# Where the arena begins in SBUF: from a multiple of 128 bytes to 64 bytes behind one

## Time and profile before

| what | value |
|---|---|
| runs shown | 2211.77, 2220.5, 2219.2 us; median 2219.2 |
| the profiled execution | 2212.16 us, its span 2210.4 us |
| TensorE's granted clock, mean | 0.985 |
| TensorE busy | 2096.7 us (95%) |
| VectorE, ScalarE busy | 779.8 us (35%), 627.7 us (28%) |
| read from HBM | 722.44 MB, 327 GB/s over the span |

### The profile page before, as it was taken

One profiled execution on the slowest core, in us unless ns is written; L12 is line 12 of the kernel. 1 busy time (PEld: TensorE's weight loads), 2 busy tenths in 40 slices (PEclk: granted clock), 3 DMA queues, 4 the chain that ended last, 5 costly groups with the idle time before them and its releaser, 6 DMA issues.

```text
span 2210.4 us, 27209 instructions
## 1 busy us (share of the span) xinstructions
PE 2096.7 (95%) x12031; PEld 1305.4 (59%) x12031; DVE 779.8 (35%) x1144; ACT 627.7 (28%) x988; POOL 42.9 (2%) x75
## 2 busy tenths in 40 slices
PE   9999999899898999989999899889999999999999
PEld 9986543333333443424333333327988998988997
DVE  8984211011010111111011011016666665876663
ACT  6664110000000000000000000005555444865442
POOL 3201000000000000000000000000000000000000
PEclk9999999999999999999999999999999999999999
DMA  7549999999999999999999999997444655544653
GB/s 239 169 137 372 425 429 429 429 429 429 429 429 430 429 430 429 429 428 428 430 429 429 430 429 429 429 427 262 147 168 148 214 191 188 193 172 149 204 191 114
DMA packets 146816, 725.27 MB, mean 328 GB/s; under 512 B 8711, under 2 KB 106555, under 8 KB 119691
## 3 DMA queue, kind: packets, MB, share of 16 engines
q1 hardware_dynamic: 145512, 721.53, 81.4%
q0 software_dynamic: 640, 1.37, 0.2%
q10 hardware_dynamic: 546, 0.63, 0.1%
HBM read 722.44 MB, written 1.07 MB: 327 GB/s over the span
## 4 chain that ended last, share of the span: by engine, by line
PE 66%; DMA 26%; DVE 5%; ACT 1%; issue 1%; SPq 0%; DVEq 0%; ACTq 0%
PE bank L1425 23%; PE bank L1287 18%; DMA weight_ring<-in_w_up_dram 10%; DMA weight_ring<-in_w_down_dram 10%; PE bank L1373 8%; PE bank L1250 5%; DMA weight_ring<-in_w_gate_dram 4%; PE bank L1456 3%; DVE weights_ring L2517 1%; DVE arena L2577 1%; PE bank L1093 1%; PE bank L1214 1%; PE bank L1642 1%; PE bank L1772 1%; PE bank L1665 1%
## 5 line engine op out<-in xcount | busy, mean ns | idle before, releaser
L1287 PE MATMUL bank<-weight_ring,arena 128*64 128x506 f32 x3024 | 633.1, 563 | 56.9 <-DMA weight_ring<-in_w_up_dram 42.5
L1287 PEld LDWEIGHTS bank<-weight_ring,arena 128*64 128x64 f32 x3024 | 219.0, 135 | 453.6 <-issue 359.3
L1373 PE MATMUL bank<-weight_ring,arena 128*64 128x512 f32 x1408 | 334.5, 628 | 36.4 <-DMA weight_ring<-in_w_down_dram 36.4
L2953 DVE TENSOR_TENSOR weights_ring<-weight_ring,weights_ring 128x2048 fp32r<-128x2048 f32 x110 | 249.7, 2289 | 127.2 <-ACT weights_ring L2211 126.8
L1373 PEld LDWEIGHTS bank<-weight_ring,arena 128*64 128x64 f32 x1408 | 102.5, 143 | 247.3 <-issue 194.3
L1425 PE MATMUL bank<-input_high,weights_ring 128*128 128x256 f32 x1920 | 242.6, 279 | 0.6 <-issue 0.6
L1425 PEld LDWEIGHTS bank<-input_high,weights_ring 128*128 128x128 f32 x1920 | 229.2, 188 | 2.7 <-issue 2.4
L2211 ACT ACTIVATE weights_ring<-weight_ring 128x2048 fp32r<-128x2048 f32 x109 | 205.7, 1909 | 61.0 <-DMA weight_ring<-in_w_ffn_down_dram 40.4
L2910 DVE TENSOR_TENSOR arena<-arena,bank 128x512 f32<-128x512 f32 x48 | 33.0, 688 | 498.2 <-PE bank L1250 498.2
L2105 ACT ACTIVATE arena<-bank 128x506 f32<-128x506 f32 (+1 forms) x48 | 23.5, 562 | 375.2 <-PE bank L1287 375.2
L1425 PE MATMUL bank<-input_low,weights_ring 128*128 128x256 f32 x960 | 129.4, 277 | 0.0
(11 more groups left out here) (432 smaller groups left out, 2079.1 us busy)
## 6 DMA issues: line engine op xcount, KB each, us to landing
weight_ring<-in_w_down_dram SPq DMA_DIRECT2D x62, 2816.0 KB, 21.8
weight_ring<-in_w_up_dram SPq DMA_DIRECT2D x60, 2816.0 KB, 19.5
weight_ring<-in_w_gate_dram SPq DMA_DIRECT2D x59, 2816.0 KB, 18.8
weight_ring<-in_w_ffn_gu_dram SPq DMA_DIRECT2D x44, 1024.0 KB, 5.1
weight_ring<-in_w_ffn_down_dram SPq DMA_DIRECT2D x22, 1024.0 KB, 4.9
weight_ring<-in_w_in_dram SPq DMA_DIRECT2D x16, 1024.0 KB, 6.3
arena<-in_w_xkv_dram SPq DMA_DIRECT2D x8, 2048.0 KB, 21.7
weight_ring<-in_w_gate_dram SPq DMA_DIRECT2D x10, 1408.0 KB, 10.0
```

Of the source, the lines that this page charges most:

```text
L1287: last = pe.matmul(bank[first_bank + c][MPAD * half:MPAD * half + MPAD, 0:(hi - lo) * HF], xs3[:, s, :], w[:, lo:hi, HF * half:HF * half + ...
L1373: last = pe.matmul(bank[6][MPAD * half:MPAD * half + MPAD, :], hidT[:, at:at + MPAD], W[:, j * D + 512 * half:j * D + 512 * half + 512], s ...
L2953: dve.tensor_tensor(low_slot(k), raw_slot(k), high_slot(k), ALU.subtract).then_inc(S("weights_low"), 1)
```

## The change

The padding ahead of the arena grows from 24 to 40 columns, from 96 to 160 bytes per partition. Every address of the arena, and of what is laid over it, rises by 64 bytes. Nothing else is different.

```diff
         RW = sb("router_w", KT * 16)
         small = sb("small", 184)
-        sb("arena_offset", 24)
+        sb("arena_offset", 40)
         Z = sb("arena", ARENA)
```

## The result

| | before | after |
|---|---|---|
| median of 10 executions | 2217.23 us (2210.87 to 2220.5) | 2225.61 us (2224.43 to 2227.12) |
| the profiled execution, its span | 2212.16, 2210.4 us | 2224.93, 2223.1 us |
| granted clock, mean | 0.985 | 0.986 |

The change makes the kernel slower by 8.4 us between the medians. That is just inside the 0.5% that the prediction set as what can be told from no change, but ten executions of each tell it apart.

The account below looks back on a forecast made before the run. It took weight transfers to bound the expert stage and TensorE the last stage. All terms were 0, so no change from the profiled 2212.16 us; the median was put at 2216 us, range 2203 to 2233 us.

Parts of the forecast that it names:

- What bounds each stage: Expert stage bound by weight transfers at 429 GB/s, last stage by TensorE multiplications one for one; first 250 us mixed.
- Transfers: Loads into the arena, mostly eight of 2048 KB in the expert stage: 0, bounds ±0.5 us.
- VectorE and ScalarE: Their arena accesses, in the last stage and first 250 us: same speed at both phases, 0, bounds ±2 us.
- full fp32: TensorE multiplications of L1642 and L1772: 379 ns whether operands share a phase modulo 128 bytes or not, so 0.
- the expert stage's slack: TensorE's waits for transfers there, 56.9 us before L1287, cover any slower multiplication: 0, or 6 us without cover.
- Rounded fp32: Last-stage TensorE multiplications of 256 and 512 columns, in_part, token_part and others: taken as 0 between bounds.
- The upper bound: Most the last stage's rounded multiplications could lose: +9.7 us for in_part, +3.3 us for 512 columns.
- Slow everywhere: All in_part multiplications of the last stage at the slow pace: 2880 x 0.75 x 4.5 ns = +9.7 us.
- The first rival: L1425, 256 columns: in_part falls into the slow pace, +13.0 us, 2229 us; chance 0.19, 0.16 over the bound.
- its worse form: In_part slow plus a further 4.5 ns on all 3456 multiplications of 256 columns: +27 us, chance 0.05.
- The second rival: Last stage: equal phases give back half the overhead of 256- and 512-column multiplications, 19 us, 2197 us; chance 0.12.
- The third: Last stage: slow stretches of in_part and token_part become fast, nothing else; -5.8 us, 2210 us; chance 0.07.

Follow-up runs that it names:

- second profile of before: Unchanged kernel profiled once more, nothing changed against before: one execution, 2214.75 us.
- The last experiment: Changed kernel with input_high and input_low moved to distance 192 from the ring, everything else at 0: 2209.13 us, 0.9975 of the kernel before.

## Why the prediction was wrong

**What bounds each stage: right.** Of 12.7 us between the spans the last stage has all, one for one as foretold. No wait grew; one of 1.0 us in the profile of before was missing in that of after, as in the second profile of before.

**Transfers, VectorE and ScalarE, full fp32, the expert stage's slack: right at 0.** 429 GB/s; 684 and 687 ns; 379 ns twice; 1127.66 against 1127.39 us. L1772, whose operands did change their distance, has 379 ns in the profiles of all six distances.

**Rounded fp32: wrong, and this is the step.** It reads "Between them I take 0, since the rows that do compare the phases (fp32, 512 columns) show nothing." The runs put +14.1 us in its place: in_part +15.6, token_part +1.1, 512 columns -2.6. Three things were wrong in it. The rows it trusted were of the kinds that hardly care: full fp32 does not move by a nanosecond, and 512 columns at 230 ns move by 1 to 3 ns, where 256 columns at 113 move by up to 6.7. The nearest row in kind and size, token_part at 117.5 ns, was named and not taken. And two paces at one address were read as "the phase does not fix the pace". It does not fix it at distance 192; at 0 it does, at 120.0.

**The upper bound was too low in one term and wrong in sign in another.** "Slow everywhere" was priced at before's slow pace, 117.9 ns, +9.7 us for in_part; it was +15.6, since the new pace was one that no row of before showed. The share of three quarters at the fast pace was right (2133 of 2880). The 512 columns, bounded at -1.6 to +3.3 us, gave -2.6: also mixed_high, counted as untouched, gained 3 ns.

**The first rival was the case that came.** In_part did become slow everywhere. Its +13.0 us meets the 13.1 of the last stage, by errors that cancel, which is luck: 5.9 us too little for in_part and 5.9 too much for the 512 columns; token_part's 1.1 us was not in it, nor the 1.0 us of the wait that went. The sign given for it, 2.83 us for 24, did not come either; it was 2.88, which no rival had. The price of its worse form, +27, is also mis-added: 13.0 and 3456 x 4.5 ns = 15.6 are 28.6. Its 2229 us did not come out, because it was laid on 2216, a guess at the median. An execution at the median already has a long run at the slow pace, and loses less. Laid on the profiled execution, 2212.16 + 13.0 is 2225.2, and 2225.61 was measured. The range (2203 to 2233) held the time; the likeliest case, no change, did not happen.

**The second rival** (equal phases let both streams pass) is refuted for 256 columns and true in small for 512: of 17 ns lost on each, 3 came back. **The third**, all fast, is not what the change does. The last experiment came nearest to it, with other addresses: both long runs are fast and 2267 of in_part's 2880 multiplications start the next one after 113 or 114 ns, but shorter stretches at 117.8 ns stayed.

**The rule of the Trainium skill** (SBUF — State Buffer, Who interferes with whom), that PE has two independent read ports and never waits on anyone, was read by the prediction as exactly 0 for this change. The section speaks of one engine against another, and there the trace agrees: the pace did not move with what VectorE, ScalarE and the DMAs did. It says nothing of where PE's own two operands lie against each other, and that cost 6.7 ns per multiplication. Whether its two reads are as independent as it says for rounded fp32, no run here shows directly, but the dependence speaks against it.

## What to carry to other kernels

Where a chain of short rounded multiplications (256 columns) bounds a kernel, the address of the moving operand less that of the stationary one, modulo 256 bytes, was worth up to 6% of their pace here: measure the pace from the timeline at several distances, and place each pair by itself, since kinds that move 256 and 512 columns want different distances. Two paces of the same instructions in one profile, or heaps in the times of one kernel, were the sign of such a dependence here, and it was read as a reason against one; lay the sum on the execution whose paces you counted. A symmetric placement, everything behind the same phase, is not better for being so.

## What the hardware showed that I had not expected

- The pace of a rounded multiplication depends on the distance of its operands modulo 256 bytes, in steps of at most 32: between 113.3 and 120.0 ns for 256 columns, 227.1 and 232.9 for 512. Moving both operands together by 64 bytes changes nothing (1.0001, 0.9989 to 1.0012).
- The kinds disagree: distance 0 is the worst for 256 columns moving from the arena and the best for 512 moving from the ring. The direction is not the reason: token_part, 256 columns moving from the ring like the 512, has its worst at 0 too (120.1 ns) and its best at 64 (113.3), where the 512 columns take 232.1 against 227.1 at 0. That leaves the size, or the order in which the kinds alternate.
- At distance 192 the same instructions at the same addresses have two paces, 113.3 and 117.8 ns, and a run keeps the one that it has. Which one a run takes can differ between the layers of one execution and between executions, and it makes a scatter of 9 us. Distance 64 has the same two, in_part mostly at the slow one. There nine executions spread over 7 us (2216.87 to 2223.86), and the profiled one was the slowest of them. Distance 128 has two as well: 118.7 ns in the long runs and 120.0 in the 168 multiplications from 1922.50 us on:

```profile
1925.38 2.08 PE L1425 MATMUL bank<-input_high,weights_ring 128*128 128x256 f32 x16
...
1928.26 2.08 PE L1425 MATMUL bank<-input_high,weights_ring 128*128 128x256 f32 x16
```

- The mixer's rounded multiplications, 272 columns, hardly changed (L894 with mixer_low, in the arena, 288 ns before and 287 after). Each of its eight tiles begins 1,088 bytes behind the last, 64 modulo 256, so that the distances rotate whatever the arena does. Mixer_high_b, one tile alone in the arena, did change, 291 to 286 ns, as its distance went from 128 to 192. That this is the reason is argued and not tried.
- Open: what in the read of the two operands collides (the stream of the moving one and the loading of the next weights are the candidates), and what picks the pace at distances 192 and 64.
